# MLA attention softmax: the four row sums of a head inverted in one VectorE instruction after the last exponential, in place of one inversion behind each exponential

## What is computed

```python
def causal_softmax_attention(q, k, v):          # 16 heads, 512 tokens, q and k 96 wide, v 64 wide
    def one(args):                              # one block of 128 query rows
        qi, bi = args
        logits = jnp.einsum('bhqd,bhkd->bhqk', qi, k) * scale
        mask = s_idx[None, :] <= t_idx[:, None]
        w = jax.nn.softmax(jnp.where(mask, logits, -jnp.inf), axis=-1)
        return jnp.einsum('bhqk,bhkd->bhqd', w.astype(v.dtype), v)
    return _unblocks(lax.map(one, (qb, jnp.arange(nb))))
```

## Time and profile before

| what | value |
|---|---|
| median of 3 runs | 1390.02 us (1389.33 to 1391.25) |
| the profiled execution, its own time | 1386.24 us |
| its span, first to last instruction | 1384.1 us |
| TensorE matmul busy | 1333.3 us, 96% of the span |
| VectorE busy | 779.3 us, 56% |
| ScalarE busy | 615.3 us, 44% |
| GpSimd busy | 322.9 us, 23% |
| MLA attention, first score product to last probability transpose | 150.3 to 261.7 us |
| mean granted TensorE clock | 0.989 of full speed |

### The profile page before, as it was taken

How to read it: one execution, slowest core, us unless ns; L and a number is a source line. 1 busy time by engine, 2 the same in 40 slices (tenths; PEclk the granted TensorE clock), 3 DMA queues, 4 the chain that set the end, 5 groups by cost and what they waited for, 6 DMA issues and landing times. The chain is left out here.

```text
span 1384.1 us, 18256 instructions
## 1 busy us (share of the span) xinstructions
PE 1333.3 (96%) x6486; PEld 1102.3 (80%) x6486; DVE 779.3 (56%) x1236; ACT 615.3 (44%) x1100; POOL 322.9 (23%) x353
## 2 busy tenths in 40 slices
PE   6999999999999999899999999799999999989997
PEld 6888677788888887788888888688888888878876
DVE  5454788733752234788444634945467236467734
ACT  4337766424532324798243423114234224345534
POOL 3104843000000005674000000920000000577610
PEclk9999999999999999999999999999999999999999
DMA  5413000022223222000323333131333322311011
GB/s 158 133 56 124 31 0 0 31 92 91 91 97 101 92 91 77 15 0 31 137 91 92 122 92 106 52 101 61 96 98 107 107 92 63 106 31 47 31 61 61
DMA packets 60314, 106.11 MB, mean 77 GB/s; under 512 B 3460, under 2 KB 16472, under 8 KB 59864
## 3 DMA queue, kind: packets, MB, share of 16 engines
q1 hardware_dynamic: 58784, 98.91, 22.6%
q0 software_dynamic: 1376, 6.27, 1.5%
q10 hardware_dynamic: 88, 0.03, 0.0%
HBM read 103.11 MB, written 2.10 MB: 76 GB/s over the span
## 5 line engine op out<-in xcount | busy, mean ns | idle before, releaser
L1424 DVE TENSOR_TENSOR w_lo<-stage,w_hi 128x1024 fp32r<-128x1024 f32 (+4 forms) x188 | 242.0, 1287 | 455.0 <-ACT w_hi L943 454.9
L943 ACT ACTIVATE w_hi<-stage 128x1024 fp32r<-128x1024 f32 (+4 forms) x188 | 191.9, 1021 | 514.8 <-PE ps L440 514.5
L438 PE MATMUL ps<-a0h,w_hi 128*128 128x512 f32 x576 | 229.6, 399 | 11.4 <-DVE w_lo L1424 8.0
L439 PE MATMUL ps<-a0l,w_hi 128*128 128x512 f32 x576 | 225.9, 392 | 0.0
L440 PE MATMUL ps<-a0h,w_lo 128*128 128x512 f32 x576 | 225.9, 392 | 0.0
L2003 POOL TENSOR_TENSOR small<-small 128x16 f32<-128x16 f32 (+2 forms) x15 | 33.4, 2226 | 537.8 <-DVE small L1502 398.2
L438 PEld LDWEIGHTS ps<-a0h,w_hi 128*128 128x128 f32 x576 | 109.1, 189 | 37.6 <-DVE w_lo L1424 10.4
L438 PE MATMUL ps<-w_hi,a0h 128*128 128x512 f32 (+1 forms) x320 | 122.8, 384 | 5.0 <-DVE w_lo L1424 5.0
L440 PEld LDWEIGHTS ps<-a0h,w_lo 128*128 128x128 f32 x576 | 109.1, 189 | 23.3
L439 PEld LDWEIGHTS ps<-a0l,w_hi 128*128 128x128 f32 x576 | 109.2, 190 | 21.5 <-issue 0.2
L440 PE MATMUL ps<-w_hi,a0l 128*128 128x512 f32 (+1 forms) x320 | 120.9, 378 | 0.0
(11 more groups left out here) (287 smaller groups left out, 2711.2 us busy)
## 6 DMA issues: line engine op xcount, KB each, us to landing
stage<-in_a_w_in SPq DMA_DIRECT2D x48, 512.0 KB, 3.8
stage<-in_ple_w_gate SPq DMA_DIRECT2D x16, 512.0 KB, 3.3
stage<-in_w_kv_shared SPq DMA_DIRECT2D x16, 512.0 KB, 3.5
stage<-in_sb_w_in SPq DMA_DIRECT2D x16, 512.0 KB, 3.6
stage<-in_a_w_out SPq DMA_DIRECT2D x16, 512.0 KB, 3.4
stage<-in_b_w_in SPq DMA_DIRECT2D x16, 512.0 KB, 3.8
stage<-in_mla_w_in SPq DMA_DIRECT2D x8, 512.0 KB, 3.7
stage<-in_mla_w_out SPq DMA_DIRECT2D x8, 512.0 KB, 3.4
```

The source lines that it names most:

```text
L438: pe.matmul(bank, wh, mh, start=start, stop=False)
L439: pe.matmul(bank, wh, ml, start=False, stop=False)
L943: act.activation(slab(w_hi[r % 2], L, nk, w), slab(stage[r % 4], L, nk, w), ACT.Copy).then_inc(S("hi_ready"), 1)
L1424: dve.tensor_tensor(slab(w_lo[r % 2], L, nk, w), slab(stage[r % 4], L, nk, w), slab(w_hi[r % 2], L, nk, w), ALU.subtract)\
```

## The change

`normalize` waits once, for all four blocks of the head, inverts the four columns of `ssum` in one instruction, and then multiplies the four blocks one behind the other, in the same order as before. The number of chain marks in a pass of the loop falls from 16 to 10. Nothing else is changed.

```diff
@@ -1668,9 +1668,9 @@
         def normalize(h):
-            for r, j in enumerate(reversed(range(MB))):
-                dve.wait_ge(S("exp_done"), MB * h + (r + 1))
-                link(dve.reciprocal(rsum[:, j:j + 1], ssum[:, j:j + 1]))
+            dve.wait_ge(S("exp_done"), MB * h + MB)
+            link(dve.reciprocal(rsum, ssum))
+            for j in reversed(range(MB)):
                 at = slice(QRY_COL[j], QRY_COL[j] + (j + 1) * P)
                 dve.tensor_scalar(pr[:, at], pr[:, at], rsum[:, j:j + 1], None, ALU.mult).then_inc(S("p_ready"), 1)
 
@@ -1712,7 +1712,7 @@
         with dve.Fori(1, PAIRS - 1) as i:
-            link.begin(i, 1, 16)
+            link.begin(i, 1, 10)
             mla_pair(i)
```

## The result

The changed kernel took 1413.18 us (median of 4 runs, 1411.5 to 1415.78) against 1389.87 us before (median of 4): ratio 1.0168, 95% interval 1.0147 to 1.0188. That is 23.3 us slower, 1.7%. The direction was forecast; the size, 14.6 us, was not, and the time lies 0.2 us above the range.

A forecast was written before the change was run, and what follows sets the result against it. TensorE was taken to bound the kernel: 15.9 us of later transposes less 1.3 us given back is 14.6 us, putting the median at 1404.6 us (slower by 1.05%). The range was 1400 to 1413 us.

The forecast's parts named there:

- E: The moment at which the fourth row sum of a head is written; the forecast counted its times from there.
- the sum: Forecast total over 16 heads: 15.9 us of later transposes less 1.3 us given back, 14.6 us slower.
- Rivals 2 and 3: VectorE is the bound, 1380.9 us, chance 0.04; or TensorE comes late anyhow, no change, 1390 us, chance 0.05.
- with 0.49 us to run: Duration taken for a head's first multiplication (512 columns) on VectorE, behind the one inversion.
- rows 5: Earlier trace's multiplication durations on VectorE: 0.285 us for 128 columns, 0.489 us for 512.
- the 1.3 us that the sum gave back: Lag of the first maximum behind the scores expected to go, 0.21 us in each of six pairs of heads.
- Rival 1: TensorE's new pause before the probability transposes halves its clock; up to 1.5 us a fall, 1412 or 1429 us, chance 0.11.
- the 1.11 us of idle time in head 0: TensorE's idle time ahead of head 0's key transposes in the kernel before, where the clock stayed 1.00; held against a fall.
- five heads of rival 1: Case in which the clock falls in five heads: 7 us more, 1412 us.
- an upper bound of the inversion: Four-column inversion on VectorE costing up to 0.48 us more a head, 7.7 us over 16 heads, 1412.3 us.
- a rival's middle case: The clock falling to half in five heads, 1412 us, between one fall and falls in all sixteen.

The follow-up runs named there:

- pool_late: Changed kernel, with GpSimd preparing a head only once the current head's ten probability transposes are done; 1407.72 us, ratio 1.0119 to the kernel before.
- head0_old: Changed kernel, with head 0 alone normalized as in the kernel before; 1412.57 us, ratio 1.0156 to the kernel before.
- head0_only: Kernel before, with head 0 alone normalized as in the changed kernel; 1394.81 us, ratio 1.0031 to the kernel before.
- two_and_two: Changed kernel, with two inversions of two columns a head, behind the second and fourth exponentials; 1394.95 us, ratio 1.0043 to the kernel before.
- wait_only: Changed kernel, keeping the wait for all four exponentials but inverting column by column ahead of each multiplication; 1421.83 us, ratio 1.0214 to the kernel before.
- pool_late_head0_old: Changed kernel, with GpSimd's preparation behind the probability transposes and head 0 normalized as before; 1401.81 us, ratio 1.0086 to the kernel before.

## Why the prediction was right and wrong

**Right.** What bounds the stage, and the first-order mechanism: TensorE, which had started the transposes ahead of E, now waits behind it (16.6 us of waits on line 1675 in 15 heads). The wide inversion costs nothing more (0.18 us). The first transpose starts at E + 0.79 where GpSimd is out of the way, against E + 0.85 in the sum; ten transposes end at E + 2.10, as the sum for head 8 had it. With both found costs taken away the stage grew by 14.3 us in 15 heads, where the sum had 13.6. The loss of a head adds to the next, and passes whole into the layer behind. Rivals 2 and 3 are out.

**Wrong, first term: the multiplications.** The steps that fail are the first multiplication "with 0.49 us to run" and, behind it, "by the same overlap and the durations of rows 5" the last one ending "some 0.8 us behind the first". In head 8 the first takes 0.67 us and the last ends 1.12 us behind it. The durations of the earlier trace rows came from multiplications that mostly ran while GpSimd idled. Moved behind E they fall on GpSimd's start: GpSimd, released by the key transposes, starts within 0.3 us of the fourth row sum (226.88 against 226.64 in head 8, 234.85 against 234.91 in head 9). Line 1675 then takes 1.78 to 1.98 us a head in heads 4 to 12, in place of 1.27. The prediction asked of GpSimd only whether it had slack; it has, and that is why its cost was missed: it is not late, it is in the way. Measured by pool_late: 4.3 us of stage. In this lies most of the 1.3 us that the sum gave back: behind head 8 the first maximum still came 1.47 us after the scores (228.90 to 230.37), and 1.28 us with GpSimd late (226.37 to 227.65), where the sum had 1.22.

The Trainium skill has the rule (SBUF — State Buffer, Who interferes with whom): VectorE and GpSimd share one pair of ports, whoever starts first holds it for the whole instruction, and tensor_scalar is among the VectorE operations that can take it. The trace agrees in its main point, since both sides lengthen: GpSimd's product of line 2026 takes 0.64 us in head 8 and that of line 2027 0.50 us in head 9 beside the multiplications, against 0.46 and 0.32 us in pool_late behind them. That it is the port, and not another shared thing, no run here shows.

**Wrong, second term: the clock.** Rival 1 came true in one head; the forecast itself had the clock at no cost. The prediction held the 1.11 us of idle time in head 0 against it, since the clock had stood that pause. It should have added the new pause to it: head 0 is the one head where TensorE waits ahead of the key transposes **and** now behind them. head0_old and head0_only put the fall there from both sides; its cost in the profiled execution of the changed kernel was 3.3 us, or 3.8 by the account below, where rival 1 had up to 1.5 us for a fall, since this one lasted 10 us and not 3. In heads 2 to 15 of the changed kernel pauses of 0.8 to 1.3 us left the clock alone, so five heads of rival 1 were too many. That two pauses are what it takes is not shown: two_and_two kept the clock with two shorter ones in head 0, and wait_only lost it once behind a single one. The Trainium skill's rule that transposes do not count like matmuls (TensorE: Matmul & The Clock Gate, Part 4: PE-mode transpose) is not settled by these traces: the busy time ahead of the fall was nearly all transposes (1.28 of the 1.51 us), but in head 0 of the kernel before TensorE did nothing but transposes from 153.0 to 157.3 us, busy for 2.79 of 4.29 us, and the clock stayed.

**The account.** Step by step from the stage of the kernel before: 14.3 us for the wait in 15 heads (to the 125.6 us of pool_late_head0_old), 4.8 us for head 0, its own wait of about 1.0 us and the clock (to the 130.5 us of pool_late), 4.3 us for GpSimd (to 134.8 us). That is the 23.4 us. Taken in the other order, over head0_old, GpSimd is 4.9 us and head 0 4.3 us. Each stage is that of one execution.

**The range** ended at 1413 us, by an upper bound of the inversion that was far off (7.7 us against nothing) and by a rival's middle case. That the time came within 0.2 us of it is luck, for it nearly held by the wrong terms: of the two costs that came, the clock was given as a case of its own and not on top of the forecast's own upper end, and GpSimd was not given at all.

## What to carry to other kernels

Merging small instructions was not free here, though it took 4 us of work off VectorE. It can be free only if the merged one does not wait for the last of its inputs; where a consumer starts on the first part early, compare the moment at which the last input arrives with the moment at which the consumer starts, and count all the work that moves behind it. When work moves in time, ask also what runs beside it in its new place: an engine with much slack can still slow its neighbour, and the durations of the old place no longer hold. And add a new pause of TensorE to the pauses that already stand around it, head by head or tile by tile, before taking the clock for granted; one row in which it stood a pause does not settle the next.

## What the runs showed of the hardware

- A VectorE tensor_scalar on fp32 tiles in SBUF beside GpSimd's copies and products takes up to 787 ns (changed kernel) where it takes 488 ns at most without them (pool_late).
- An inversion of 128x4 elements takes 0.18 us, one of 128x2 0.17 us, one of 128x1 0.16 us (changed kernel, two_and_two, kernel before).
- Behind a stretch in which TensorE was busy for 1.51 of 3.50 us the granted clock went to one half for about 10 us (changed kernel, head 0); in head0_only, behind 0.83 of 3.40 us, for 3.4 us. TensorE was busy for 9.57 of the 10.50 us in the first of them.
